# Output norm by PSUM halves on two engines, fewer filler products, a reordered first stage and a weight queue two loads further ahead, in a three-layer block on one core

## What is computed

```python
sh1, sc1, gt1, sh2, sc2, gt2 = split(silu(c) @ w_mod + b_mod, 6)
h = rms_norm(x, g_pre_mix) * (1 + sc1) + sh1          # the context likewise
mix = token_mix(h, hc, w_in, ...)                     # retention heads and an RWKV scan, both directions
x = x + gt1 * rms_norm(mix, g_post_mix)
h2 = rms_norm(x, g_pre_ffn) * (1 + sc2) + sh2
# 16 experts, each takes the 32 tokens with the highest affinity to it
affinity = softmax(h2 @ w_router); gate_vals, tok_idx = top_k(affinity.T, 32)
ye = (silu(xs @ w_gate[e]) * (xs @ w_up[e])) @ w_down[e] * gate_vals
x = x + gt2 * rms_norm(scatter_add(ye, tok_idx), g_post_ffn)
# then twice: mixing (four kinds of heads) and a gated feed-forward of width 2816, and a final rms_norm
```

## Time and profile before

| | us |
|---|---|
| median of 3 runs | 1829.65 (1828.99 to 1830.1) |
| profiled execution | 1836.64 |
| its span on the core | 1834.6 |
| TensorE (PE) busy | 1645.0 (90%) |
| VectorE (DVE) busy | 727.8 (40%) |
| ScalarE (ACT) busy | 371.8 (20%) |
| GpSimd (POOL) busy | 77.2 (4%) |

### The profile page before, as it was taken

The page is one execution under the profiler, slowest core; times in us unless marked ns, Lnnn a source line. Parts: engine busy times, 40 slices in busy tenths (PEclk is TensorE's granted clock), DMA queues, the critical chain, the costliest instruction groups (busy, mean ns, idle before and its releaser), DMA issues.

```text
span 1834.6 us, 29021 instructions
## 1 busy us (share of the span) xinstructions
PE 1645.0 (90%) x12736; PEld 1064.6 (58%) x12736; DVE 727.8 (40%) x1326; ACT 371.8 (20%) x870; POOL 77.2 (4%) x94
## 2 busy tenths in 40 slices
PE   9999998988999876676666999999999999999998
PEld 5665557948835322121112386769984577679963
DVE  2005465675563100000000235556664255646663
ACT  2110133544422201010000224320010225210000
POOL 0000003304220000000000000000000000000000
PEclk9999998998998999888888999999999999999999
DMA  8621020040086999999999932224454532135450
GB/s 368 252 100 47 11 110 2 4 184 3 4 346 265 429 430 431 430 430 431 430 430 431 397 149 92 92 92 179 150 224 180 205 132 72 68 120 202 184 195 23
DMA packets 35583, 381.90 MB, mean 208 GB/s; under 512 B 6977, under 2 KB 10433, under 8 KB 12673
## 3 DMA queue, kind: packets, MB, share of 16 engines
q1 hardware_dynamic: 35458, 380.04, 51.2%
HBM read 378.98 MB, written 1.05 MB: 207 GB/s over the span
## 4 chain that ended last, share of the span: by engine, by line
PE 45%; DMA 17%; DVE 3%; ACT 2%; issue 1%; DVEq 0%; PEldq 0%
DMA arena<-in_w_moe 17%; PE psum L2959 15%; PE psum L3021 7%; PE psum L2340 6%; PE psum L2343 3%; PE psum L2009 2%; PE psum L162 2%; PE psum L2493 2%; PE psum L2481 1%; PE psum L2041 1%; PE psum L1976 1%; PE psum L2460 1%; PE psum L1956 1%; PE psum L2369 0%; PE psum L2446 0%
## 5 line engine op out<-in xcount | busy, mean ns | idle before, releaser
L2959 PE MATMUL psum<-arena 128*128 128x128 f32 x1408 | 165.2, 275 | 1.7 <-DVE arena L3157 1.7
L2959 PEld LDWEIGHTS psum<-arena 128*128 128x128 f32 x1408 | 161.0, 192 | 2.0 <-issue 2.0
L2157 DVE COPY arena<-psum 128x512 f32<-128x512 f32 x16 | 11.1, 691 | 373.2 <-PE psum L2009 373.2
L2959 PE MATMUL psum<-arena,weight_ring 128*128 128x128 f32 x1056 | 127.9, 277 | 6.3 <-DVE arena L3195 4.2
L2959 PEld LDWEIGHTS psum<-arena,weight_ring 128*128 128x128 f32 x1056 | 123.4, 194 | 8.6 <-issue 5.8
L1371 PE MATMUL psum<-arena 64*64 64x64 f32 x3328 | 109.0, 222 | 10.9 <-POOL arena L1542 8.1
L2340 PE MATMUL psum<-arena,weight_ring 128*128 128x256 f32 x512 | 118.5, 382 | 0.3 <-ACT arena L2555 0.3
L1371 PEld LDWEIGHTS psum<-arena 64*64 64x64 f32 x3328 | 101.5, 137 | 17.3 <-POOL arena L1542 8.6
L2340 PEld LDWEIGHTS psum<-arena,weight_ring 128*128 128x128 f32 x512 | 94.5, 189 | 19.1 <-issue 2.9
L2009 PE MATMUL psum<-arena 128*32 128x512 f32 x480 | 68.4, 701 | 36.8 <-DMA arena<-in_w_moe 36.8
L3140 DVE TENSOR_TENSOR arena<-weight_ring 128x1024 f32<-128x1024 f32 (+1 forms) x72 | 81.2, 1128 | 51.0 <-PE psum L3021 51.0
(11 more groups left out here) (498 smaller groups left out, 2333.7 us busy)
## 6 DMA issues: line engine op xcount, KB each, us to landing
weight_ring<-in_w_moe SPq DMA_DIRECT2D x50, 2048.0 KB, 44.9
arena<-in_w_moe SPq DMA_DIRECT2D x46, 2048.0 KB, 44.3
weight_ring<-in_w_in SPq DMA_DIRECT2D x23, 2048.0 KB, 11.4
weight_ring<-in_w_mod SPq DMA_DIRECT2D x12, 2048.0 KB, 11.8
weight_ring<-in_w_gate SPq DMA_DIRECT2D x12, 2048.0 KB, 7.9
weight_ring<-in_w_up SPq DMA_DIRECT2D x12, 2048.0 KB, 7.9
weight_ring<-in_w_down SPq DMA_DIRECT2D x12, 2048.0 KB, 7.9
weight_ring<-in_w_out SPq DMA_DIRECT2D x6, 2048.0 KB, 7.8
```

The lines of the kernel that those rows point to most:

```text
L2959: last = nc.tensor.matmul(K.ps[:, bank, P * n:P * n + P], lhs, rhs, start=(n == 0 and k == 0 and name in ("m1", "m5", "m6")), stop=(k == 3 ...
```

## The change

1. **First stage.** The bias products of the first two column sets move ahead of the first partial product; the two `combine` of sets 0 and 1 stand together behind the second partial product; the half projection is cut into four quarters, which stand between the later partial products and combines. Ten fillers instead of thirteen stand at the start, one filler and a wait at the end go. The bias row and the gain are loaded ahead of the first weight slot.
2. **Slot count.** `load_ahead(sp, 7)` becomes `load_ahead(sp, 9)` in `project_and_retain`, and so the queue is two loads further ahead in every later stage.
3. **Output norm.** The square is taken in two halves of one PSUM bank each, while VectorE multiplies the other half by gt1; the root comes in with the addition of x. The second tile is squared before ScalarE copies the first tile's transposed rows.
4. **Fillers.** Fewer at the second turn (3 to 1), ahead of the transposes in routing (1 to 0), behind them (8 to 6), and in the last expert (of 10 ahead of its last product, 3 stay).
5. **Mixing.** VectorE rotates before it waits for the tables, and the two exponentials move behind the first jobs.

```diff
-                W.load_to(sp, 1)
...
-                def warm(count, width=4):
+                def warm(count, width=4, bank=0):
                     for _ in range(count):
-                        nc.tensor.matmul(K.ps[:, 1, 0:P * width], K.ones, K.ones.unsqueeze(1).broadcast_to([P, width, P]),
+                        nc.tensor.matmul(K.ps[:, bank, 0:P * width], K.ones, K.ones.unsqueeze(1).broadcast_to([P, width, P]),
...
-                def combine(c):
-
-                    pe.wait_ge(in_rows, 32)
+                to = lambda c, b: K.ps[:, 2 + c % 2, 2 * b:2 * b + 2]
+
+                def add_bias(c):
                     if c >= 2:
                         pe.wait_ge(mod_kept, c - 1)
-                    to = lambda b: K.ps[:, 2 + c % 2, 2 * b:2 * b + 2]
                     for b in range(4):
                         at = 512 * columns[c] + P * b
-                        nc.tensor.matmul(to(b), brow[0:1, at:at + P], K.ones[0:1, 0:2], start=(b == 0), stop=False, skip_group_check=True)
+                        nc.tensor.matmul(to(c, b), brow[0:1, at:at + P], K.ones[0:1, 0:2], start=(b == 0), stop=False, skip_group_check=True)
+
+                def combine(c):
+
                     pe.wait_ge(part_kept, c + 1)
                     for b in range(4):
-                        last = nc.tensor.matmul(to(b), part[:, c % 2, P * b:P * b + P], K.sel, start=False, stop=True,
+                        last = nc.tensor.matmul(to(c, b), part[:, c % 2, P * b:P * b + P], K.sel, start=False, stop=True,
                                                 skip_group_check=True)
                     last.then_inc(mod_made, 1)
+
+                def half_projection(b):
+                    for k in range(4):
+                        last = nc.tensor.matmul(K.ps[:, 4 + b, 0:T], K.first_projection[:, k, P * b:P * b + P], K.hT[:, k, T:2 * T],
+                                                start=(k == 0), stop=False, skip_group_check=True)
+                        if b == 0 and k == 0:
+                            last.then_inc(W.used, 1)
...
-                warm(13)
+                warm(10)
+                pe.wait_ge(in_rows, 32)
+                add_bias(0)
+                add_bias(1)
                 pe.wait_ge(cond_ready, 2)
                 partial(0, W.take(pe), None)
                 pe.wait_ge(in_ident, 16)
                 for j in range(4):
                     turn(j)
+                partial(1, W.take(pe), W.used)
                 pe.wait_ge(sel_ready, 1)
                 combine(0)
-                partial(1, W.take(pe), W.used)
                 combine(1)
                 K.first_projection = W.take(pe)
+                warm(2, 2, 0)
                 pe.wait_ge(latent_scaled["dve"], 3)
                 pe.wait_ge(latent_scaled["act"], 1)
-                for b in range(4):
-                    for k in range(4):
-                        last = nc.tensor.matmul(K.ps[:, 4 + b, 0:T], K.first_projection[:, k, P * b:P * b + P], K.hT[:, k, T:2 * T],
-                                                start=(k == 0), stop=False, skip_group_check=True)
-                        if b == 0 and k == 0:
-                            last.then_inc(W.used, 1)
+                half_projection(0)
                 partial(2, W.take(pe), None)
+                add_bias(2)
+                add_bias(3)
+                half_projection(1)
                 combine(2)
-                warm(2, 2)
                 partial(3, W.take(pe), None)
+                half_projection(2)
                 combine(3)
-                keep_busy(nc, K, 0, 1)
-                pe.wait_ge(mod_made, 4)
+                half_projection(3)
...
-                W.load_ahead(sp, 7)
+                W.load_ahead(sp, 9)
...
-    sums, ms, scales = A.temp(4), A.temp(4), A.temp(4)
+    sums, ms, scales = A.temp(6), A.temp(4), A.temp(4)
     h2T = K.mixT
     pair = lambda ap, n: ap[:, 2 * n:2 * n + 2]
     wide = lambda n: K.ps[:, n, :].rearrange("p (h t) -> p h t", t=T)
     half = (slice(0, HD), slice(HD, P))
     part_bank = (0, 2, 1, 3)
+    half_of = lambda ap, n: ap[:, 512 * n:512 * n + 512]
     var_bank, gate_bank, fold_bank = (4, 6, 4, 6), (5, 7, 5, 7), (4, 6)
-    mixed = lambda t: K.ps[:, 2 * t:2 * t + 2, :].rearrange("p a b -> p (a b)")
...
-                keep_busy(nc, K, 1, 3)
+                keep_busy(nc, K, 1, 1)
...
+                def square_mix(t):
+                    act.wait_ge(mix_made, t + 1)
+                    for n in range(2):
+                        if n == 1:
+                            act.wait_ge(mix_taken, 2 * t + 1)
+                        nc.scalar.activation(half_of(junk[:, t, :], n), K.ps[:, 2 * t + n, :], ACT.Square,
+                                             accum_out=sums[:, 2 * t + n:2 * t + n + 1]).then_inc(mix_squared, 1)
+
+                square_mix(0)
                 for t in range(TT):
-                    act.wait_ge(mix_made, t + 1)
-                    nc.scalar.activation(junk[:, t, :], mixed(t), ACT.Square, accum_out=sums[:, t:t + 1]).then_inc(mix_squared, 1)
                     act.wait_ge(mean_ready, 2 * t + 1)
                     nc.scalar.activation(scales[:, t:t + 1], ms[:, t:t + 1], ACT.Sqrt).then_inc(root_ready, 1)
                     act.wait_ge(x_ready, t + 1)
-                    nc.scalar.activation(junk[:, t, :], K.x[:, t, :], ACT.Square, accum_out=sums[:, 2 + t:3 + t]).then_inc(mix_squared, 1)
+                    nc.scalar.activation(junk[:, t, :], K.x[:, t, :], ACT.Square, accum_out=sums[:, 4 + t:5 + t]).then_inc(mix_squared, 1)
                     act.wait_ge(mean_ready, 2 * t + 2)
                     nc.scalar.activation(scales[:, 2 + t:3 + t], ms[:, 2 + t:3 + t], ACT.Sqrt).then_inc(root_ready, 1)
-                    if t == 1:
+                    if t == 0:
+                        square_mix(1)
+                    else:
...
-                    dve.wait_ge(mix_squared, n + 1)
-                    nc.vector.tensor_scalar(ms[:, at:at + 1], sums[:, at:at + 1], 1.0 / D, EPS, ALU.mult, ALU.add).then_inc(mean_ready, 1)
                     dve.wait_ge(root_ready, n + 1)
                     link(nc.vector.reciprocal(scales[:, at:at + 1], scales[:, at:at + 1]))
 
+                def take_mix(t):
+                    dve.wait_ge(mix_made, t + 1)
+                    for n in (1, 0):
+                        if n == 0:
+                            dve.wait_ge(mix_squared, 3 * t + 1)
+                        nc.vector.tensor_tensor(half_of(mix[:, t, :], n), K.ps[:, 2 * t + n, :], half_of(gt1, n),
+                                                ALU.mult).then_inc(mix_taken, 1)
+                    dve.wait_ge(mix_squared, 3 * t + 2)
+                    link(nc.vector.tensor_tensor(ms[:, t:t + 1], sums[:, 2 * t:2 * t + 1], sums[:, 2 * t + 1:2 * t + 2], ALU.add))
+                    nc.vector.tensor_scalar(ms[:, t:t + 1], ms[:, t:t + 1], 1.0 / D, EPS, ALU.mult, ALU.add).then_inc(mean_ready, 1)
+
                 dve.wait_ge(x_in_landed, 16)
                 dve.wait_ge(gt1_ready, 1)
+                take_mix(0)
                 for t in range(TT):
                     inverse_root(2 * t, t)
-                    link(nc.vector.scalar_tensor_tensor(mix[:, t, :], mixed(t), scales[:, t:t + 1], gt1, ALU.mult, ALU.mult))
-                    nc.vector.tensor_tensor(K.x[:, t, :], x_in[:, t, :], mix[:, t, :], ALU.add).then_inc(x_ready, 1)
+                    dve.wait_ge(mix_taken, 2 * t + 2)
+                    nc.vector.scalar_tensor_tensor(K.x[:, t, :], mix[:, t, :], scales[:, t:t + 1], x_in[:, t, :],
+                                                   ALU.mult, ALU.add).then_inc(x_ready, 1)
+                    dve.wait_ge(mix_squared, 3 * t + 3)
+                    nc.vector.tensor_scalar(ms[:, 2 + t:3 + t], sums[:, 4 + t:5 + t], 1.0 / D, EPS, ALU.mult, ALU.add).then_inc(mean_ready, 1)
                     inverse_root(2 * t + 1, 2 + t)
+                    dve.wait_ge(x_ready, t + 1)
                     nc.vector.tensor_scalar(K.h2[:, t, :], K.x[:, t, :], scales[:, 2 + t:3 + t], None, ALU.mult).then_inc(normed, 1)
+                    if t == 0:
+                        take_mix(1)
...
-        keep_busy(nc, K, 1, 1)
         pe.wait_ge(aff_ready, 1)
         for t in range(TT):
             last = nc.tensor.transpose(K.ps[experts_row, 5, P * t:P * t + P], aff[:, t, :], K.ident)
         last.then_inc(affT_made, 1)
-        keep_busy(nc, K, 1, 8)
+        keep_busy(nc, K, 1, 6)
...
-            if e == NE - 1:
-                keep_busy(nc, K, 7, 2)
...
-                        keep_busy(nc, K, 7, 2)
+                        keep_busy(nc, K, 7, 1)
...
-                    if e == NE - 1:
-                        keep_busy(nc, K, 5, 2)
...
+        for name in before_units[2:]:
+            item(name)
         act.wait_ge(lam_ready, once)
         nc.scalar.activation(lsum, lsum, ACT.Exp).then_inc(lam_exp, 1)
         act.wait_ge(f_abs, once)
```

(8 more changed lines are left out.)

1 line of the change is left out of this document (added).

## The result

| | before | after |
|---|---|---|
| median | 1829.88 (4 runs, 1828.99 to 1831.28) | 1821.42 (4 runs, 1820.72 to 1824.28) |
| ratio, 95% interval | | 0.9947 (0.9930 to 0.9963) |
| profiled execution | 1836.64 | 1820.72 |
| its span | 1834.6 | 1818.6 |
| mean granted clock of TensorE | 0.959 | 0.963 |

The change gains 8.5 us by the medians and 9.7 by the ratio (0.0053 x 1829.88). The two profiled executions lie 15.9 apart, which is more than both: the profile of before was 6.8 above this median (7.0 above the one that the prediction used), that of after sits on its lowest run. This gap runs through the whole case.

The account below looks back on a forecast made before the run. The weight stream was taken to bound the experts' stage, TensorE nearly everywhere else. s = 11.4, with 1.6 and zero for F and G, gave 13.0: 1836.64 became 1823.6, less 7.0 to the median, 1816.6 us (range 1810.5 to 1823).

Parts of the forecast that it names:

- A: First stage: new order 5.0 us shorter, and the next block's slow-clock start about half removed, 1.5: -6.5 us.
- C: Outputs: no wait for the fourth modulation slot and no cold products behind it: -3.9 us.
- E: Routing: fewer fillers around the transposes hold TensorE up less: -1.3 us.
- B: Deeper queue's costs: barriers after stages two and three +0.8, stage three's late small tables +0.6: +1.4 us.
- G: Mixing, twice: earlier rotations and later small operations against tables delayed by two weight slots: 0 us (-0.3 to +1).
- slot count, behind the stream: Experts: slots 3 and 4 land before the stage ends, by itself bringing 1.6 us (0.5 to 3).
- D: Output norm: halves alternating between ACT and DVE, second tile squared earlier: -1.1 us (-0.2 to -1.6).
- F: Last expert: with fewer fillers, earlier start gains 1.2 us, colder product and scatter lose: 0 (-1.2 to +3).
- The law: Experts: if TensorE first uses slot 0 s earlier, the gain behind the weight stream is s + 1.6 us.
- My first rival: First stage keeps little, cold in its middle and at the next block's start: only -3, time 1820 us; chance 0.18.
- my last rival: Fewer fillers keep TensorE's clock low from 575 (+9) and from slot 95 (+8): slower, 1840 us; chance 0.04.

Follow-up runs that it names:

- turn_two: The changed kernel with two fillers instead of one ahead of the second turn: 1818.18 us, ratio 0.9924 to the kernel before.
- norm_only: The kernel before with the new output norm alone, its three fillers ahead of the second turn kept: 1831.41 us, ratio 1.0006 to the kernel before.
- first_only: The kernel before with the first stage's new order alone: 1826.88 us, ratio 0.9981 to the kernel before.
- queue_undone: The changed kernel with its weight queue no further ahead than before (load_ahead 7 instead of 9): 1826.51 us, ratio 0.9981 to the kernel before.
- both: The changed kernel with the projection's second quarter ahead of the third partial product and a second filler ahead of the second turn: 1817.47 us, ratio 0.9915.
- queue_only: The kernel before with the weight queue two loads further ahead and nothing else: 1831.80 us, ratio 1.0006 to the kernel before.

## Why the prediction was right, and where its terms were not

The forecast was 1816.6 with a range of 1810.5 to 1823.0. The median, 1821.42, lies in it, 4.8 above the forecast: of 13.0 us, 8.5 came (9.7 by the ratio). The way in which a gain passes on to the end was right. Most of the single terms were not, A, C and E being off by some 2 us each, and that the median still fell into a range 12.5 wide is in part luck. Term by term:

| term | predicted | shown by the runs |
|---|---|---|
| A first stage | -6.5 | -4.3 mean (-6.3 warm, 0 in two profiles of eight) |
| B deeper queue, its costs | +1.4 | 0 at the barriers; 2.7 and 4.1 in the second mixing, taken away by G |
| C fourth modulation slot | -3.9 | -0.5, -0.7, -2.2, -3.9 in four profiles: mean -1.8 |
| slot count, behind the stream | -1.6 | -1.6 (443.2 to 441.6, means of three and two profiles that lie up to 1.8 apart); -3.3 by the queue undone |
| D output norm | -1.1 | -2.0 with one filler ahead of the turn, -1.1 with three warm ones, 0 with three cold ones |
| E routing's fillers, and those of the turn | -1.3 | +1.1 |
| F last expert | 0 | 0 by the times, +0.3 to +0.6 by the profiles |
| G mixing | 0 | beside a short queue not run, nothing to be seen; -2.7 or more beside the long one |
| stages four and five | 0 | -1.5 (214.7 to 213.2, means of four and ten profiles), no part of the change is known to do it |

D and E can't simply be added, since each depends on the other's state. Taken together, from the last product of outputs to the first expert, four profiles with neither take 30.0, 28.3, 28.2 and 29.7 (mean 29.0), the changed kernel's two 28.2 and 28.4: -0.8. With -1.6 for the slot count and nothing for B, F and G together this makes -4.3 - 1.8 - 1.6 - 0.8 = -8.5, and -10.0 with stages four and five, about the 8.5 to 9.7 that were measured. The agreement is no proof: each mean comes from a few profiles that spread by as much as the term.

**The law** (s + 1.6, the stream restarts at the first use of slot 0) is right: 14.82 gave 16.30. The 1.6 in it is the least certain part, as its row in the table shows. Slot 10's issue to the last slot's first product is 1007.50 - 584.06 = 423.4; the prediction had 3.4 + 86 x 4.886 = 423.6. The hole ahead of slot 10 is there: 115 GB/s from 578 to 582 and 8 from 582 to 584, where the kernel before moved about 430 in the 12 us ahead of its slot 10.

**A** failed at "I take -5.0" and, more, at "I take about half, -1.5" for a warm start of the second block. The new order itself runs as I worked it out but for the third modulation slot, whose product starts at 29.2 to 29.4 in every profile, so that TensorE waits 1.6 to 2.7 where I had 1 (0.3 in turn_two, where the quarter ahead of it ran cold, 3.49). What I didn't see is that the old stage loses 3 us or more to the lower clock in each of its four profiles, only in changing places; removing the place that one profile showed would not have removed the loss. That the new order removes it in three of its eight profiles, hides it in the wait for the slot in one (turn_two) and doubles it in two came out of the experiments. My first rival (the first stage keeps little) names this; the chance of 0.18 was too small, since a quarter of the profiles is its case and another quarter in between.

**C** failed at its size. 2.14 of wait, 0.77 and 0.99 were rows of one execution (0.88 rather than 0.99: warm, the product behind takes 1.13). In norm_only the same wait is 2.17 with nothing cold behind it, in first_only and queue_undone it is 0.64 and 0.39. Why the slot lands 12.9 to 14.7 behind its issue there stays open. The two slots of w_out are issued right behind it in all four, and three slots at 4.886 would be 14.7; no run separates them.

**D** was too small for the norm itself, which is 1.9 shorter to the second turn, because I charged the alternating halves and VectorE's copy ahead of the root: +0.5 and some of the copy's 0.7. The root is ready only at 555.94 and VectorE's copy has ended by 556.3, so that the copy costs 0.3 and the halves nothing that is seen. What I did not say is that fillers decide how much of it passes: in the profile that I read they stood as long as the old norm took, because they were cold, and with three warm ones the 1.1 that I forecast is what passed.

**E** failed at "end at 590 to 591, against slots ready at 588.8". I took "two or three of them cold" and the turn as "may run cold, 0.6 each way: 0". They ran cold from the turn on: 0.93 in the turn, 1.6 behind it, and the six fillers still end behind VectorE (576.82 against 575.45). That was my last rival's mechanism, the clock from 575 on, at far less than its 9 us: the clock was back before the gather. Of the lower clock where a short burst follows a wait for data, the last products of the last expert speak once more: in six of the eight profiles with few fillers there the last one takes 3.3 to 3.5 instead of 1.92, and in the other two, turn_two and both, the one ahead of it takes 3.57 and 3.58 and the last 1.92. The rule of the Trainium skill that the prediction quotes ("TensorE: Matmul & The Clock Gate", section "HAM oscillation — how this bites in real kernels"), by which that is so every time, holds for the last product in six of the eight. The +1.5 for F that the prediction worked out by it did not come, since the product starts earlier, as the run with the fillers back shows.

**The step from the profile to the median** failed. I took the sum, 13.0, from an execution 7.0 above its median and carried the 7.0 over. But part of those 7.0 lay in the very places that the change removes: the cold product of C (1.76 of its 3.9), the extra cold of the three fillers (4.52 against 2.82 in queue_only and first_only), the cold start of block two. An execution at the median can't have had all of them to lose. That is argued and not shown, since no execution of the kernel before near its median was profiled. The outputs of the profile took 92.01 to the first expert; in first_only, whose code is the same there, 88.51.

**B and G** failed as reasons, though not in their sum. I looked for the price of the deeper queue at the barriers and in stage three, and found nothing there (65.18 in all profiles). It lies far behind, in the second mixing, near 1447. For the first mixing I had the mechanism in hand ("Two weight slots, 9.8 us, come ahead of the tables, which land near 1059"), and took the wait as hidden; that it would be on the path in the second layer without the reorder I didn't work out.

## What to carry to other kernels

Where a program's profile shows stretches at the lower clock, take a second and a third profile before pricing them: in the old first stage they cost 3 us or more in each of four executions but sat in different places, and an edit gets rid of the place and not always of the loss. Don't add such a term to a profile that lies above its median and then carry the distance over; a part of it is counted twice. When fillers fill a wait, shorten them together with what they cover and measure both: of the norm's 2.0 us the fillers of before hid one half or all, and one filler too few cost 3.3. And a deeper load queue has its price where small tables are issued behind it, far from the slots that it helps; look for the engine that stands at a wait for those tables with copies for TensorE behind it in its list.

## What the runs showed of the hardware that I had not expected

- One and the same program up to the end of the first stage starts its second block at 43.0 to 43.2, 44.7 to 44.8 or 49.5 to 49.6, by where TensorE's granted clock falls to its lower level: not at all or in a place that a wait hides, for a few us from 28 on, or from there to 44. The first part of `rwkv_latent`, the same code in all, takes 38.6 to 39.2 in nine profiles and 40.5 to 43.7 in five, by a cold stretch at its first partial product. Times of one kernel spread by as much: 1825.84 to 1834.58 in 35 runs of the kernel before.
- Where no cold stretch falls, everything repeats to hundredths: stage two takes 174.80 us in twelve of fourteen profiles, stage three 65.17 to 65.19 in all of them.
- ScalarE and VectorE in neighbouring banks of PSUM at the same time slow each other by nothing that shows: 0.60 and 0.7 for 128x512 each, as elsewhere in the trace.
